# Linear attention's forget sums in two rounded passes, and attention's low weight halves one step later

## The chip, the cores and the metric

The kernel runs on one core of one Trainium2 chip. Time is device microseconds of one execution; lower is better. Before the change the median of 3 runs is 3329.88 us (3328.59 to 3332.18).

## The reference

Two transformer blocks follow one another on 512 tokens of width 1024. The first has 16 extra meta tokens (528 positions that count) and two layers. Each layer projects its input to four branches: windowed attention with a sink (A), attention with axial rotation (B), differential attention (C), and a gated linear attention (D) in both directions. Their outputs are weighed by gates and summed; a feed-forward follows. The second block has a feed-forward, attention with a state space model, and another feed-forward. The change touches only the first block; what matters of it:

```python
def gates(z, lb):
    f = lb + (1.0 - lb) * jax.nn.sigmoid(z)
    log_f = jnp.log(jnp.maximum(f, F_FLOOR))      # the forget logarithms
    kk = (1.0 - lb) * jax.nn.sigmoid(-z) * vmask
    return log_f, kk

def step(S, inp):                                  # one chunk of the linear attention
    qi, ki, vi, gi = inp                           # gi: log_f of the chunk
    b = jnp.cumsum(gi, axis=2)                     # sums of forget logarithms
    diff = b[:, :, :, None, :] - b[:, :, None, :, :]
    decay = jnp.where(tri, jnp.exp(jnp.where(tri, diff, 0.0)), 0.0)
    attn = jnp.einsum('bhtk,bhtsk,bhsk->bhts', qi, decay, ki)
    o = jnp.einsum('bhts,bhsv->bhtv', attn, vi) + jnp.einsum('bhtk,bhkv->bhtv', qi * jnp.exp(b), S)
    b_last = b[:, :, -1:, :]
    S = S * jnp.exp(b_last[:, :, 0, :, None]) + jnp.einsum('bhsk,bhsv->bhkv', ki * jnp.exp(b_last - b), vi)
    return S, o
```

## The kernel before

All engines have a program of their own, written out in order; semaphores join them. Nothing is scheduled by a planner: where an instruction stands in its engine's list is where the code puts it, by step numbers.

Most products are made in three rounded passes (type fp32r). A weight `w` is split into a high half, which ScalarE copies with rounding (`high_weights`, L1608), and a low half, which VectorE makes as weight minus high half (`low_weights`, L2026); inputs are split likewise. TensorE then adds high x high, high x low and low x high (L1040 to L1042; L1302 to L1304 for the gates). Unrounded fp32 matmuls appear as two records each in the trace.

A layer of the first block runs so:

1. Norm; then six products `fm[0..5]` with feature rows (weights w[0..5]). The first two are staged (`staged_lin`): all high x high first, then low weights, then low inputs. In layer 0 three small products for bias rows follow the second.
2. Products `tm` with token rows, for (i, t): i = 0, 1, 2 and five tiles t (four of 128 tokens, one of 16). ScalarE reads each from the accumulator (L1902 for i = 2). Tiles i = 0, 1 give the gates; GpSimd floors them; `forget_logs` runs on ScalarE in two passes over LZ (square root, L1851, and logarithm, L1848), after tiles 1 and 3 of i = 2.
3. Attention in steps n: first the C steps from c0, then A from a0, then B from b0. In a step TensorE makes scores, VectorE minima (L2147, L2163), ScalarE exponentials (L1679), TensorE turns and multiplies (L1205), ScalarE and VectorE copy and mix results (L1693, L2213); step n works on parts of attention n, n-1, n-2, n-3. The rest of the projections (weights w[12..21]) is put between as "fill" on TensorE, and their weights are split in given steps (`splits_at`), on ScalarE and VectorE in the same step n. From step b0+6 on, `gate_splits` prepares the first gate weights in the same way.
4. `linear_attention`: ten units (five tiles, two directions) per layer. In each, TensorE turns the keys (L1420), makes Z (L1422) and for each of two head pairs the `sums` (L1345): a matrix R of zeros and ones times the forget logarithms LZ, both fp32, with 128 rows and 2 x 512 columns. An exponential, the pair products on VectorE, and further small products follow. Between them stand gate pieces (`fill`).
5. Output product and feed-forward.

Of the kernel before, what the change touches and what calls it, by code (L numbers as in the profile page):

```python
# [23 lines left out]
P = 128  # L24
# [223 lines left out]
def build(nc, ins, out_dram):  # L248
    with ExitStack() as ctx:
# [134 lines left out]
        u6 = 4960  # L384
        XMH = [XR[:, base + (4 + i) * L:base + (5 + i) * L] for i in range(6)]
# [75 lines left out]
        names += """gate_floored dz_gate dz_log state_cleared g_sums g_exp g_kf g_query_x g_key_x g_z g_ez  # L461
# [126 lines left out]
        for l in range(DEPTH):  # L588
# [7 lines left out]
            for i, source in enumerate((FAQ, FAQ + 1, FCQ, FCQ + 1, FAK, FCK)):  # L596
                ly["w"].append(early(ins["w_fm"][l, source], KT, P))
                ly["fm"].append(split_job(ly["w"][-1], range(KT), 0, xu, FULL))
                if l == 0 and i == 1:
# [183 lines left out]
        for ly in layers:  # L783
# [5 lines left out]
            for n, i in ((c0 + 2, 14), (c0 + 3, 15), (a0, 16), (a0, 17), (a0 + 2, 18), (a0 + 3, 19), (b0, 20), (b0 + 1, 21)):  # L789
                splits_at.setdefault(n, []).append(ly["w"][i])  # L790
# [3 lines left out]
            split_from[ly["l"]] = b0 + 6  # L794

# [229 lines left out]
        def _(pe):  # L1025
# [291 lines left out]
            def linear_attention(ly):  # L1317
# [3 lines left out]
                pe.wait_ge(S["dz_log"], NT * (l + 1))  # L1321
# [18 lines left out]
                def sums(n, hp):  # L1340
# [73 lines left out]
                for n in range(NUNIT):  # L1414
# [51 lines left out]
            def first_block():  # L1466
                for ly in layers:
                    l = ly["l"]
                    mean_square(ly["norm"])
                    staged_lin(ly["fm"][0:2], ly["xu"])  # L1470
                    if l == 0:
                        bias_rows()
                    for j in ly["fm"][2:]:
                        split_lin(j)
# [99 lines left out]
        def _(act):  # L1574
# [159 lines left out]
            def attention(first, end, ly=None):  # L1734
                for n in range(first, end + 2):
# [130 lines left out]
            def first_block():  # L1866
                for ly in layers:
                    l = ly["l"]
                    if l == 0:
                        squares(ly["norm"])  # L1870
                        for ld in ly["w"][0:2]:
                            high_weights(ld)
                    else:
                        root(ly["norm"])
                        act.wait_ge(S["h_stored"], 64)
                    high_tiles(ly["xu"])
                    high_weights(ly["w"][2])
                    for i, j in enumerate(ly["fm"]):
# [9 lines left out]
                        if l == 0 and i in (1, 3, 5):  # L1888
                            (bias_rows, start_exp, start_lambda)[i // 2]()
# [3 lines left out]
                    for i, t, j in ly["tm"]:  # L1893
                        full(act, j)
                        acc_t, c = PB[j.buf][0:j.rows, 0, 0:CG], CG * (i % 3)
                        if i < 2:
                            A(KTM[0:j.rows, t, c:c + CG], acc_t, ACT.Sigmoid, scale=-1.0)
                            A(LZ[0:j.rows, t, c:c + CG], acc_t, ACT.Sigmoid).then_inc(S["tm_ready"], 1)
                            if (i, t) in ((0, 1), (1, 2), (1, 3)):
                                high_weights(ly["w"][(9, 8 + t)[i]])  # L1900
                            continue
# [892 lines left out]
```

## Time and profile before

| | |
|---|---|
| median of 3 runs | 3329.88 us |
| profiled execution, its own time | 3336.33 us |
| its span | 3334.2 us |
| mean granted TensorE clock | 0.955 |
| TensorE busy | 3094.7 us (93%) |
| VectorE busy | 1771.0 us (53%) |
| ScalarE busy | 1006.5 us (30%) |
| GpSimd busy | 218.8 us (7%) |
| L1345 (sums), 128 rows | 66.1 us busy, 128 records |

The span is the profiled execution's, and its own time contains a little more around it. Busy time of TensorE is modelled at the ends of matmuls, so that neighbours overlap in the rows; the distance from one start to the next is what a matmul holds the engine. A window row gives the length of a stretch and what each engine was busy in it, with the clock granted to TensorE (1.00 is full speed).

### The profile page before, as it was taken

How to read it: one execution, taken by the hardware profiler on the slowest of the kernel's cores; microseconds unless marked ns; L12 is line 12 of the kernel's file. 1: busy time of each engine (PE TensorE's matmuls, PEld its weight loads, DVE VectorE, ACT ScalarE, POOL GpSimd, SP SyncE). 2: the span in 40 equal slices, each digit the busy share in tenths (PEclk: the TensorE clock that was granted, in tenths of full speed). 3: DMA queues.
4: the chain of work that ended last, by engine and by line, in shares of the span. 5: the costliest groups of instructions: out<-in, count | busy, mean ns of one | idle time of the engine just before them, and what ended most of it. 6: DMA issues, size and time to landing. Idle time of an engine off the chain costs nothing.

```text
span 3334.2 us, 51815 instructions
## 1 busy us (share of the span) xinstructions
PE 3094.7 (93%) x21724; PEld 2610.9 (78%) x21724; DVE 1771.0 (53%) x3315; ACT 1006.5 (30%) x1728; POOL 218.8 (7%) x455
## 2 busy tenths in 40 slices
PE   8888999999999998889999999989999797889997
PEld 7766888999999896778888788867888454558886
DVE  4463476547646436446755775646446425453334
ACT  4554222232212235432223222233222114332221
POOL 0120211100000100212110000000000000000000
PEclk9988899999999999989999999989999898899998
DMA  5201111134534420111114453412334210213231
GB/s 180 88 14 45 41 57 57 64 129 146 175 106 130 134 72 31 38 41 57 57 56 138 149 177 122 149 60 89 114 113 170 91 45 1 70 59 105 89 102 69
DMA packets 74494, 302.47 MB, mean 91 GB/s; under 512 B 10728, under 2 KB 11112, under 8 KB 69272
## 3 DMA queue, kind: packets, MB, share of 16 engines
q1 hardware_dynamic: 57880, 230.04, 21.4%
q0 software_dynamic: 16384, 69.13, 5.8%
q8 instruction: 173, 2.83, 0.4%
q14 instruction: 57, 0.47, 0.0%
HBM read 288.51 MB, written 14.63 MB: 91 GB/s over the span
## 4 chain that ended last, share of the span: by engine, by line
PE 84%; DVE 9%; ACT 5%; issue 2%; DMA 0%; POOL 0%; DVEq 0%; ACTq 0%; SPq 0%
PE acc L1040 17%; PE acc L1041 17%; PE acc L1042 17%; PE acc L1302 5%; PE acc L1303 5%; PE acc L1304 5%; PE acc L1074 3%; PE acc L1345 2%; PE acc L1205 2%; PE acc L1179 1%; DVE work L1975 1%; ACT temps L1679 1%; DVE normed L1993 1%; PE acc L1366 1%; PE acc L1089 1%
## 5 line engine op out<-in xcount | busy, mean ns | idle before, releaser
L1041 PE MATMUL acc<-normed_r,toep_r 128*128 128x512 f32 (+1 forms) x1824 | 644.2, 353 | 0.0
L2026 DVE TENSOR_TENSOR ring_r<-ring,toep_r 128x1024 fp32r<-128x1024 f32 (+2 forms) x340 | 458.6, 1350 | 298.2 <-ACT toep_r L1608 297.8
L1608 ACT ACTIVATE toep_r<-ring 128x1024 fp32r<-128x1024 f32 (+2 forms) x340 | 392.7, 1157 | 710.4 <-PE acc L1042 709.6
L1041 PEld LDWEIGHTS acc<-normed_r,toep_r 128*128 128x128 f32 x1824 | 345.5, 189 | 46.2 <-issue 0.2
L1040 PE MATMUL acc<-work_r,toep_r 128*128 128x512 f32 (+1 forms) x1024 | 354.0, 346 | 6.5 <-DVE temps_r L2017 6.3
L1042 PE MATMUL acc<-work_r,ring_r 128*128 128x512 f32 (+1 forms) x1024 | 353.0, 345 | 0.0
L1040 PE MATMUL acc<-mixed_r,toep_r 128*128 128x264 f32 (+1 forms) x1056 | 343.9, 326 | 5.1 <-DVE ring_r L2026 4.4
L1042 PE MATMUL acc<-mixed_r,ring_r 128*128 128x264 f32 (+1 forms) x1056 | 340.1, 322 | 0.0
L1040 PE MATMUL acc<-temps_r,toep_r 128*128 128x512 f32 x768 | 305.0, 397 | 24.3 <-DVE normed_r L2012 14.8
L1302 PE MATMUL acc<-residual_r,toep_r 128*128 128x264 f32 (+1 forms) x1024 | 316.0, 309 | 1.6 <-DVE mixed L2213 1.6
L1041 PE MATMUL acc<-work_r,toep_r 128*128 128x512 f32 (+1 forms) x880 | 307.3, 349 | 0.0
L1042 PE MATMUL acc<-temps_r,ring_r 128*128 128x512 f32 x768 | 302.1, 393 | 0.0
L1303 PE MATMUL acc<-normed_r,toep_r 128*128 128x264 f32 (+1 forms) x1024 | 293.6, 287 | 0.0
L1304 PE MATMUL acc<-residual_r,ring_r 128*128 128x264 f32 (+1 forms) x1024 | 292.3, 285 | 0.0
L1040 PEld LDWEIGHTS acc<-work_r,toep_r 128*128 128x128 f32 x1024 | 192.7, 188 | 31.9 <-issue 6.9
L1040 PEld LDWEIGHTS acc<-mixed_r,toep_r 128*128 128x128 f32 x1056 | 200.0, 189 | 20.2 <-issue 5.2
L1042 PEld LDWEIGHTS acc<-mixed_r,ring_r 128*128 128x128 f32 x1056 | 200.2, 190 | 15.7
L1042 PEld LDWEIGHTS acc<-work_r,ring_r 128*128 128x128 f32 x1024 | 192.9, 188 | 24.4
L1302 PEld LDWEIGHTS acc<-residual_r,toep_r 128*128 128x128 f32 x1024 | 197.5, 193 | 15.4 <-issue 8.5
L1303 PEld LDWEIGHTS acc<-normed_r,toep_r 128*128 128x128 f32 x1024 | 197.2, 193 | 7.9 <-issue 7.9
L1304 PEld LDWEIGHTS acc<-residual_r,ring_r 128*128 128x128 f32 x1024 | 197.4, 193 | 0.0
L1040 PEld LDWEIGHTS acc<-temps_r,toep_r 128*128 128x128 f32 x768 | 145.5, 189 | 64.5 <-issue 25.1
(389 smaller groups left out, 5438.1 us busy)
## 6 DMA issues: line engine op xcount, KB each, us to landing
ring<-in_w_pair SPq DMA_DIRECT2D x176, 512.0 KB, 3.5
ring<-in_w_down SPq DMA_DIRECT2D x64, 704.0 KB, 4.1
ring<-in_w_gb SPq DMA_DIRECT2D x64, 640.0 KB, 3.9
extra<-in_w_ada POOLq DMA_DIRECT2D x18, 1024.0 KB, 5.7
toep<-in_w_ada POOLq DMA_DIRECT2D x18, 1024.0 KB, 5.5
ring<-in_w_tm SPq DMA_DIRECT2D x24, 512.0 KB, 3.8
ring<-in_w_out SPq DMA_DIRECT2D x24, 512.0 KB, 3.5
ring<-in_w_fm SPq DMA_DIRECT2D x20, 512.0 KB, 4.0
```

Of the source, the lines that this page charges most:

```text
L1040: mm(out, wh, xh[:, a:z], start=i == 0, stop=False)
L1041: mm(out, wh, xl[:, a:z], start=False, stop=False)
L1042: last = mm(out, wl, xh[:, a:z], start=False, stop=end)
L1074: last = mm(PB[j.buf][0:j.rows, s, 0:z - a], w, x[:, a:z], start=i == 0, stop=i == len(j.terms) - 1)
L1089: last = mm(n["acc"][:, s, :], mean[P * len(n["tiles"])], x[:, a:z], start=i == 0, stop=i == len(n["tiles"]) - 1)
L1205: last = mm(PS[64 * j:64 * j + 64, 6, P * i:P * i + rows], v, x, start=b == 0, stop=b == k - 1, skip_group_check=True)
L1302: mm(out, wh, xh[:, a:z], start=m == 0, stop=False)
L1303: mm(out, wh, xl[:, a:z], start=False, stop=False)
L1304: last = mm(out, wl, xh[:, a:z], start=False, stop=m == len(xs) - 1)
L1345: last = mm(PS[:, i, :].rearrange("p (l t) -> p l t", l=4)[:, :, 0:rows], LZ[0:rows, t, 256 * d + P * hp:256 * d + P * hp + P], R[d][0:row ...
L1608: A(high(ld), slot(ld), ACT.Copy).then_inc(S["w_high"], 1)
L2026: V.tensor_tensor(low(ld), slot(ld), high(ld), ALU.subtract).then_inc(S["w_low"], 1)
```

## The change

- `sums` and `Z` take the logarithms as a high half LZH and a low half LZL and the 0/1 matrices in rounded type: two rounded passes for each matmul. The matrices are rounded in place by ScalarE once, in layer 0 (two copies of 128x1152). The log halves are made by `high_log` (ScalarE) in steps b0+1 to b0+5, and `low_log` (VectorE) one step later, five tiles each.
- Low weight halves and the low parts of `gate_splits` are made on VectorE one attention step after the high halves. w[16] and w[17] are split a step earlier on ScalarE (a0-1).
- `forget_logs` stands after tiles 0 and 2, and the splits of w[12] and w[13] after tiles 1 and 2.
- At a layer's start three products are staged; bias rows follow the third; w[2] is split with w[0] and w[1] (layer 0), or before the root and the tiles (layer 1).

```diff
@@ tensor engine @@
-                    staged_lin(ly["fm"][0:2], ly["xu"])
+                    staged_lin(ly["fm"][0:3], ly["xu"])
...
                     for i in range(2):
-                        last = mm(PS[:, i, :].rearrange("p (l t) -> p l t", l=4)[:, :, 0:rows],
-                                  LZ[0:rows, t, 256 * d + P * hp:256 * d + P * hp + P],
-                                  R[d][0:rows, 4 * i:4 * i + 4, 0:rows], start=True, stop=True)
+                        for x in (LZH, LZL):
+                            last = mm(PS[:, i, :].rearrange("p (l t) -> p l t", l=4)[:, :, 0:rows],
+                                      x[0:rows, t, 256 * d + P * hp:256 * d + P * hp + P],
+                                      RR[d][0:rows, 4 * i:4 * i + 4, 0:rows], start=x is LZH, stop=x is LZL)
                     last.then_inc(S["g_sums"], 1)
...
-                    mm(PS[0:rows, 5, 0:256], Z[d][0:rows, 0:rows], LZ[0:rows, t, 256 * d:256 * d + 256],
-                       start=True, stop=True).then_inc(S["g_z"], 1)
+                    mm(PS[0:rows, 5, 0:256], ZR[d][0:rows, 0:rows], LZH[0:rows, t, 256 * d:256 * d + 256],
+                       start=True, stop=False)
+                    mm(PS[0:rows, 5, 0:256], ZR[d][0:rows, 0:rows], LZL[0:rows, t, 256 * d:256 * d + 256],
+                       start=False, stop=True).then_inc(S["g_z"], 1)
@@ attention steps @@
-            for n, i in ((c0 + 2, 14), (c0 + 3, 15), (a0, 16), (a0, 17), (a0 + 2, 18), (a0 + 3, 19), (b0, 20), (b0 + 1, 21)):
+            for n, i in ((c0 + 2, 14), (c0 + 3, 15), (a0 - 1, 16), (a0 - 1, 17), (a0 + 2, 18), (a0 + 3, 19), (b0, 20), (b0 + 1, 21)):
+            ly["log_step"] = b0 + 1
@@ scalar engine @@
+                    if ly and 0 <= n - ly["log_step"] < NT:
+                        high_log(ly["l"], n - ly["log_step"])
...
+            def high_log(l, t):
+                n = TILES[t][1] - TILES[t][0]
+                act.wait_ge(S["dz_log"], NT * l + t + 1)
+                A(LZH[0:n, t, :], LZ[0:n, t, :], ACT.Copy).then_inc(S["log_high"], 1)
...
-                        for ld in ly["w"][0:2]:
+                        for ld in ly["w"][0:3]:
                             high_weights(ld)
                     else:
+                        high_weights(ly["w"][2])
                         root(ly["norm"])
                         act.wait_ge(S["h_stored"], 64)
                     high_tiles(ly["xu"])
-                    high_weights(ly["w"][2])
...
-                        if t in (2, 3):
-                            high_weights(ly["w"][10 + t])
-                        if t in (1, 3):
-                            forget_logs(l, t == 3)
+                        if t in (1, 2):
+                            high_weights(ly["w"][11 + t])
+                        if t in (0, 2):
+                            forget_logs(l, t == 2)
@@ vector engine @@
-                    for ld in splits_at.get(n, ()) if n < end else ():
+                    for ld in splits_at.get(n - 1, ()) if first < n <= end else ():
                         low_weights(ld)
-                    if ly and n >= split_from[ly["l"]]:
+                    if ly and 0 <= n - 1 - ly["log_step"] < NT:
+                        low_log(ly["l"], n - 1 - ly["log_step"])
+                    if ly and n > split_from[ly["l"]]:
                         for i in range(2 + ly["l"]):
-                            gate_splits(ly, (n - split_from[ly["l"]]) * (2 + ly["l"]) + i)
+                            gate_splits(ly, (n - 1 - split_from[ly["l"]]) * (2 + ly["l"]) + i)
+
+            def low_log(l, t):
+                n = TILES[t][1] - TILES[t][0]
+                dve.wait_ge(S["log_high"], NT * l + t + 1)
+                V.tensor_tensor(LZL[0:n, t, :], LZ[0:n, t, :], LZH[0:n, t, :], ALU.subtract).then_inc(S["log_low"], 1)
```

TensorE (PE) in the first unit of the linear attention, before:

```order
L1420 MATMUL acc<-con,extra 128x128 x2
L1422 MATMUL acc<-work,con 128x256
L1345 MATMUL acc<-con,work 128x512 x2
L1302 MATMUL acc<-residual_r,toep_r 128x264
L1303 MATMUL acc<-normed_r,toep_r 128x264
```

The same place now:

```order
L1429 MATMUL acc<-con,extra 128x128 x2
L1431 MATMUL acc<-work_r,con_r 128x256
L1433 MATMUL acc<-work_r,con_r 128x256
L1354 MATMUL acc<-con_r,work_r 128x512 x4
L1309 MATMUL acc<-residual_r,toep_r 128x264
L1310 MATMUL acc<-normed_r,toep_r 128x264
```

One exact matmul of Z became two rounded ones, and two exact ones of the sums four; the gate pieces behind them stand where they stood.

VectorE (DVE) in the C step in which w[14] is split (L2147 minima, L2183 and L2197 the mix of the step before, L2026 the low half), before:

```order
L2147 ISA temps,small<-acc,toep,small 128x512
L2147 ISA small 128x1
L2026 TENSOR_TENSOR ring_r<-ring,work_r 128x1024
L2183 RECIPROCAL small<-small 128x4
L2186 SCALAR_TENSOR_TENSOR small<-small 128x2
L2197 SCALAR_TENSOR_TENSOR temps<-temps,small 128x528 x2
L2163 SCALAR_TENSOR_TENSOR temps<-acc,toep 128x2x16 x2
L2171 TENSOR_REDUCE small<-temps 128x4
L2147 ISA temps,small<-acc,toep,small 128x512
```

Now (L2171 minima, L2207 and L2221 the mix, L2050 the low half):

```order
L2171 ISA temps,small<-acc,toep,small 128x512
L2171 ISA small 128x1
L2207 RECIPROCAL small<-small 128x4
L2210 SCALAR_TENSOR_TENSOR small<-small 128x2
L2221 SCALAR_TENSOR_TENSOR temps<-temps,small 128x528 x2
L2187 SCALAR_TENSOR_TENSOR temps<-acc,toep 128x2x16 x2
L2195 TENSOR_REDUCE small<-temps 128x4
L2171 ISA temps,small<-acc,toep,small 128x512
...
L2050 TENSOR_TENSOR ring_r<-ring,work_r 128x1024
L2237 TENSOR_TENSOR mixed<-mixed,acc 128x2x128
```

The low half left its place ahead of the next step's reciprocal and stands behind that step's last minimum.

ScalarE (ACT) at the end of the token-major products (L1902 the reads, L1608 a high half, L1848 the pass of logarithms), before:

```order
L1902 ACTIVATE work<-acc 128x256
L1608 ACTIVATE mixed_flat_r<-ring 128x1024
L1902 ACTIVATE work<-acc 128x256
L1608 ACTIVATE mixed_flat_r<-ring 128x1024
L1848 ACT_TABLE_LOAD
L1848 ACTIVATE work<-work 128x512 x4
L1848 ACTIVATE work<-work 16x512
L1902 ACTIVATE work<-acc 16x256
```

Now (L1926 the reads, L1619 a high half, L1867 the logarithms):

```order
L1926 ACTIVATE work<-acc 128x256
L1619 ACTIVATE mixed_flat_r<-ring 128x1024
L1926 ACTIVATE work<-acc 128x256
L1619 ACTIVATE mixed_flat_r<-ring 128x1024
L1867 ACT_TABLE_LOAD
L1867 ACTIVATE work<-work 128x512 x4
L1867 ACTIVATE work<-work 16x512
L1926 ACTIVATE work<-acc 128x256
L1926 ACTIVATE work<-acc 16x256
```

Two reads stand behind the logarithms in place of one, the one of the last whole tile and the one of the tile of 16 rows.

## Rows read from the trace of the kernel before

**Rows 1.** The page, the chain that ended last, share of the span by engine.

```profile
PE 84%; DVE 9%; ACT 5%; issue 2%; DMA 0%; POOL 0%; DVEq 0%; ACTq 0%; SPq 0%
```

**Rows 2.** Windows: length, then busy and (count) of PE, PEld, DVE, ACT, POOL; clock.

```profile
116.20:342.50 226.30, 195.33 (x1719) 152.17 (x1719) 117.52 (x362) 116.17 (x323) 24.72 (x25) 0.88 0.09 29
343.00:618.00 275.00, 264.62 (x2866) 233.96 (x2866) 173.30 (x386) 71.74 (x115) 51.48 (x146) 0.96 0.17 54
...
1446.00:1718.00 272.00, 260.85 (x2891) 230.38 (x2889) 175.10 (x387) 72.62 (x117) 50.62 (x145) 0.96 0.17 55
```

**Rows 3.** Lines by form, PE: busy and mean ns, idle before.

```profile
L1345 PE MATMUL acc<-con,work 128*128 128x512 f32 x128 | 66.1, 642 | 0.0
```

**Rows 4.** Timeline of PE in the linear attention: start, length.

```profile
431.43 0.60 PE L1422 MATMUL acc<-work,con 128*128 128x256 f32 x2
431.87 1.88 PE L1345 MATMUL acc<-con,work 128*128 128x512 f32 x4
433.18 0.69 PE L1302 MATMUL acc<-residual_r,toep_r 128*128 128x264 f32 x1
...
433.83 0.28 PE L1304 MATMUL acc<-residual_r,ring_r 128*128 128x264 f32 x1
433.95 0.28 PE L1302 MATMUL acc<-residual_r,toep_r 128*128 128x264 f32 x1
```

**Rows 5.** Timeline of PE in the second block's feed-forward.

```profile
2500.14 0.39 PE L1041 MATMUL acc<-normed_r,toep_r 128*128 128x512 f32 x1
2500.37 0.39 PE L1042 MATMUL acc<-temps_r,ring_r 128*128 128x512 f32 x1
```

**Rows 6.** Timeline of PE, another block of sums.

```profile
402.73 3.30 PE L1345 MATMUL acc<-con,work 128*128 128x512 f32 x4
405.36 0.79 PE L1302 MATMUL acc<-residual_r,toep_r 128*128 128x264 f32 x1
```

**Rows 7.** Windows of C steps, the second to fourth with a split.

```profile
130.28:137.25 6.97, 6.85 (x66) 5.48 (x65) 5.04 (x15) 4.48 (x14) 0.00 (x0) 1.00 0.00 0
137.25:148.22 10.97, 8.71 (x73) 7.48 (x72) 6.18 (x16) 5.97 (x17) 0.00 (x0) 0.84 0.01 1
148.22:159.13 10.91, 8.00 (x66) 5.74 (x65) 7.13 (x20) 5.92 (x15) 0.00 (x0) 0.84 0.00 0
...
1280.69:1291.96 11.27, 8.36 (x65) 5.93 (x64) 7.49 (x20) 5.92 (x15) 0.00 (x0) 0.85 0.00 0
```

**Rows 8.** Timelines of DVE and PE there; in brackets the wait and its releaser.

```profile
139.08 1.23 DVE L2026 TENSOR_TENSOR ring_r<-ring,work_r 128x1024 fp32r<-128x1024 f32 x1 [3.47 <-ACT work_r L1608]
142.47 0.38 PE L1176 MATMUL acc<-con,temps 128*16 128x128 f32 x2 [2.26 <-DVE temps L2163]
158.43 0.18 DVE L2183 RECIPROCAL small<-small 128x4 f32<-128x4 f32 x1 [1.78 <-ACT temps L1679]
```

**Rows 9.** Timeline of PE, A steps of the first and the second layer.

```profile
220.23 0.52 PE L1179 MATMUL acc<-con,temps 128*128 128x128 f32 x3 [1.91 <-ACT mixed L1693]
1335.32 0.66 PE L1205 MATMUL acc<-mixed,work 128*64 128x128 f32 x8 [1.57 <-DVE mixed L2213]
```

**Rows 10.** Windows of B steps.

```profile
277.96:288.14 10.18, 8.31 (x62) 7.08 (x61) 3.10 (x9) 4.42 (x11) 0.00 (x0) 0.83 0.22 66
288.14:295.29 7.15, 7.15 (x70) 5.99 (x69) 2.30 (x8) 3.39 (x9) 0.00 (x0) 1.00 0.00 0
1392.93:1401.98 9.05, 6.76 (x61) 5.53 (x60) 3.33 (x9) 4.60 (x11) 0.00 (x0) 1.00 0.25 74
...
323.19:332.22 9.03, 7.11 (x38) 3.82 (x37) 3.40 (x10) 4.33 (x11) 0.00 (x0) 0.50 0.00 0
```

**Rows 11.** Timeline of PE, start of the second layer's attention.

```profile
1249.94 0.43 PE L1145 MATMUL acc<-con,work 128*128 128x64 f32 x2 [2.88 <-ACT work L1902]
```

**Rows 12.** Timeline of PE, first products of the first and the second layer.

```profile
45.02 0.39 PE L1040 MATMUL acc<-residual_r,temps_r 128*128 128x264 f32 x1 [1.09 <-ACT work L1840]
1159.81 1.12 PE L1059 MATMUL acc<-residual_r,temps_r 128*128 128x264 f32 x2 [5.97 <-ACT residual_r L1623]
```

More of the change, by code:

```diff
@@ L384, in build @@
         u6 = 4960
+        LZH, LZL = (x.rearrange("p (t c) -> p t c", t=NT) for x in (
+            XR[:, base + 4 * L:base + 4 * L + NT * 512], XR[:, z0:z0 + NT * 512]))
+        sums_at = CONSTS["R0"][0], CONSTS["Z1"][1]
+        con_r = rounded("con")
+        RR = [part(con_r, CONSTS, f"R{d}").rearrange("p (l t) -> p l t", l=8) for d in range(2)]
+        ZR = [part(con_r, CONSTS, f"Z{d}") for d in range(2)]
         XMH = [XR[:, base + (4 + i) * L:base + (5 + i) * L] for i in range(6)]
@@ L598, in build @@
                 ly["fm"].append(split_job(ly["w"][-1], range(KT), 0, xu, FULL))
-                if l == 0 and i == 1:
+                if l == 0 and i == 2:
                     bias_jobs = [job([(part(par, PARAMS, "bias_tab", 32),
@@ L1320, in linear_attention @@
                 pe.wait_ge(S["y_ready"], ly["groups"])
-                pe.wait_ge(S["dz_log"], NT * (l + 1))
+                pe.wait_ge(S["sums_rounded"], 2)
+                pe.wait_ge(S["log_low"], NT * (l + 1))
                 pe.wait_ge(S["fill_read"], NFILL * (l + 1))
@@ L1469, in first_block @@
                     mean_square(ly["norm"])
-                    staged_lin(ly["fm"][0:2], ly["xu"])
+                    staged_lin(ly["fm"][0:3], ly["xu"])
                     if l == 0:
                         bias_rows()
-                    for j in ly["fm"][2:]:
+                    for j in ly["fm"][3:]:
                         split_lin(j)
@@ L1887, in first_block @@
                         high_weights(ly["w"][i + 3])
-                        if l == 0 and i in (1, 3, 5):
-                            (bias_rows, start_exp, start_lambda)[i // 2]()
+                        if l == 0 and i in (2, 3, 5):
+                            (bias_rows, start_exp, start_lambda)[(i - 1) // 2]()
                     if l == 0:
@@ L1900, in first_block @@
                                 high_weights(ly["w"][(9, 8 + t)[i]])
+                            if l == 0 and (i, t) in ((0, 2), (0, 3)):
+                                act.wait_ge(S["consts_loaded"], 16)
+                                m = sums_at[0] + (t - 2) * (sums_at[1] - sums_at[0]) // 2
+                                w = slice(m, m + (sums_at[1] - sums_at[0]) // 2)
+                                A(con_r[:, w], con[:, w], ACT.Copy).then_inc(S["sums_rounded"], 1)
                             continue
                         A(TMt[0:j.rows, t, TAV:TAV + CG], acc_t, ACT.Copy).then_inc(S["tm_ready"], 1)
-                        if t in (2, 3):
-                            high_weights(ly["w"][10 + t])
-                        if t in (1, 3):
-                            forget_logs(l, t == 3)
+                        if t in (1, 2):
+                            high_weights(ly["w"][11 + t])
+                        if t in (0, 2):
+                            forget_logs(l, t == 2)
                     attention(ly["C"][0], ly["B"][1], ly)
@@ L2441, in start @@
                 V.tensor_tensor(lb, lb, lo, ALU.subtract).then_inc(S["lb_shift"], 1)
-                for ld in w[5:7]:
-                    low_weights(ld)
+                low_weights(w[6])
                 dve.wait_ge(S["lb_exp"], 1)
@@ L2696, in first_block @@
                     normed(ly["norm"], gain("ln_mix", l), U)
-                    if l == 0:
-                        for ld in ly["w"][0:2]:
-                            low_weights(ld)
+                    for ld in ly["w"][2 * l:3]:
+                        low_weights(ld)
                     low_tiles(ly["xu"])
-                    for ld in ly["w"][2:5]:
+                    for ld in ly["w"][3:6 - l]:
                         low_weights(ld)
```

2 lines of the change are left out of this document (1 added, 1 removed).

## The prediction

> **What bounds the kernel now.** I read first the chain of waits: 84% of the span is TensorE work, 9% VectorE, 5% ScalarE, and DMA is at 0% [rows 1]. So only what TensorE does, or what it waits for, can move the time. Then the windows by stage. In the linear attention of either layer TensorE is busy 264.62 of 275.00 us and 260.85 of 272.00, with VectorE at 173.30 and ScalarE at 71.74 [rows 2]: that stage ends with TensorE's own work, and a cheaper matmul there is worth its whole length as long as the others keep up. In the attention stage TensorE is busy 195.33 of 226.30 us [rows 2], so some 30 us per layer are waits, each followed by a stretch at a lower granted clock (0.88 over the stage). There it matters which instruction TensorE stands behind. The change touches both: cheaper sums in the first, another order of VectorE's work in the second. The queues of SyncE and GpSimd keep their order.
>
> **Part 1, the sums.** The kernel runs 128 records of L1345 with 512 columns, of 642 ns mean by the modelled ends [rows 3]; since ends are modelled I go by starts. One block of `sums` (two matmuls, four records) starts at 431.87 and what follows starts at 433.18, and the next weight-and-row group comes only at 433.95 [rows 4]. The first matmul behind the block then holds 0.77 us instead of the 0.37 that three passes of 264 columns take at 0.12 each (433.83 to 433.95) [rows 4]. So a block holds TensorE 1.31 + 0.40 = 1.71 us; as four equal records, 4 x 0.43 = 1.72. In the new kernel it is four rounded matmuls of 512 columns. One of those takes 0.23 from start to start (2500.14 to 2500.37) [rows 5]: 0.92 a block, 0.80 less. There are 32 such blocks; 28 run at full clock: 28 x 0.80 = 22.4. Four run at half (402.73 to 405.36, 2.63 us, twice the 1.31 [rows 6]) and save about 1.35 each: 5.4. Together 27.8. `Z` was two records of 256 columns in 0.44 us (431.43 to 431.87) [rows 4] and becomes two rounded ones of half of 0.23 each, 0.24: 0.2 x 16 units = 3.1. The units of 16 rows I count at 0.5 in all, as they are an eighth of the size. Linear attention: **-31.4**. Bounds: -34.6 if a block holds TensorE for the whole 1.88 us of its row (0.96 x 32 = 30.7 in place of 27.8), and +62 if a rounded pass takes as long as two exact records (rival D).
>
> TensorE would be late if the pairs on VectorE came to set the pace. They use 173.30 of 275.00 us [rows 2]; with 31.4/2 = 16 less per layer there remain about 259, still 86 above VectorE's work.
>
> On this the Trainium skill has a rule that speaks against it ("TensorE: Matmul & The Clock Gate", LDWEIGHTS (loading the stationary operand)): a load takes its columns / 1.2 in ns, an estimated 107 ns for 128 columns; were every load to show, the sum would be about 17 us smaller (4 x 0.107 x 32 + 2 x 0.107 x 16). The trace disagrees that it shows: rounded passes of 264 columns, each with a load, follow one another in 0.12 us [rows 4].
>
> **Part 2, low halves one step late.** A C step without a split lasts 6.97 us, with TensorE busy 6.85. The steps in which w14 and w15 are split last 10.97, 10.91 and, in layer 1, 11.27, at clock 0.84 or 0.85 [rows 7] (the fourth is like the first). The cause stands in rows 8: the low half starts on VectorE at 139.08 after 3.47 us of waiting for ScalarE's high half, which closes its own step; everything queued behind it (reciprocal, difference, the next minima) is late by that, and TensorE idles 2.26 us at 142.47, and then pays half clock. In the changed kernel the high half was made a step earlier, so VectorE starts it without a wait. Its own 1.23 us remain, but VectorE waits 1.78 us for ScalarE's exponentials at 158.43 anyway [rows 8], and this hides it. Four steps x (10.97 - 7.0): **-15.9**. Bounds: 0 (the wait reappears at another releaser) to -16.5.
>
> The same in the A steps: four waits of the kind of 1.91 and 1.57 us [rows 9], 6.5 in all with their clock. Half of them end with ScalarE's copies (L1693) and not with VectorE, so I take two thirds: **-4.3** (0 to -6.5). The high halves of w16 and w17 also go a step earlier on ScalarE, into the last C step; a plain one has it busy for 4.48 of 6.97 us [rows 7], so two copies fit.
>
> B steps: 10.18 against a plain 7.15 is 3.0; the step before it gives 1.2, layer 1 gives 1.9 (9.05) and 0.3 [rows 10]: **-6.4** (0 to -6.4). Gate splits at the end of B: the step of 323.19 lasts 9.03 at clock 0.50, TensorE busy 7.11 [rows 10], so 1.92 idle. Two steps of either layer are of this kind: 4 x 1.92 = **-7.7** (-2, as some of it is the end of the attention itself, to -12 with the half clock).
>
> Against that: the log halves. ScalarE copies five tiles of 512 per layer in steps b0+1 to b0+5, VectorE subtracts five, one step later. A subtraction of 1024 elements takes 1.23 us [rows 8], so half of it, 0.6 or a bit more. The Trainium skill gives for fp32 of 512 elements an estimate of (512+151)/0.96 = 691 ns ("VectorE: DVE Perf Modes", The TRN2 errata); by it the five would be 3.5 us, hidden or not as below. A plain B step has VectorE busy 2.30 and ScalarE 3.39 of 7.15 us [rows 10], so the work is covered; what is queued behind it, the first minimum or exponential of the next step, may come late by some of it. 0.2 x 10 = **+2.0** (0 to +7, if all is on the path).
>
> **Part 3, forget logs.** ScalarE's pass of logarithms (a table load and five activations) stands before the last reads of the projections, and TensorE waits 2.88 us at 1249.94 for the read behind it [rows 11], and as long in layer 0. One tile earlier, two reads follow the pass and TensorE has a tile's matmuls left meanwhile: I leave it one read's wait, an estimated 0.45, so 2 x 2.43 = **-4.8** for both layers (0 to -5.8). It now needs the floor of the gates earlier, but only one tile's time.
>
> **Part 4, starts and rounding.** In layer 0 three products are staged by halves instead of two, and ScalarE copies w[2] before the tiles. TensorE waits 1.09 at 45.02 for the bias rows' copies [rows 12]; afterwards the bias rows come one product later and w[5]'s DMA is what is waited for there: 0 (-1 to +2). In layer 1 w[2]'s high half is now before the root on ScalarE, in the chain whose end is TensorE's longest wait, 5.97 us at 1159.81 [rows 12]: **+1.0** (0 to +1.1), the 1.06 us of such a copy. The rounding of the constants (two copies of 1152 columns) is in layer 0's token-major tiles, where ScalarE has over 2 us idle per tile: 0 (to +2.3).
>
> **Sum.** -31.4 - 15.9 - 4.3 - 6.4 - 7.7 + 2.0 - 4.8 + 1.0 = -67.5. The profiled execution took 3336.33 (its span is 3334.2), so 3268.8; the median of the runs is 6.45 below it: **3262**. For this case alone I take 3252 to 3278: not all terms reach their ends together.
>
> **Rivals.** A: the waits move rather than go. VectorE's low half now stands before the step's last minima or mixes, ScalarE's exponentials become the releaser, and only a third of part 2's 34.3 is had: 23 less, **3285**. For it: ScalarE is busy 5.97 of 10.97 in a C step [rows 7] and is the releaser at 158.43. Against: plain steps of the same kind reach 6.97 with both engines.
> B: shorter sums run into the chain sums, exp, pairs, products; linear attention gives only a third, 10.5: **3283**. For it: `pairs` come directly on the sums' exp. Against: 86 us of room, and behind a block stands gate work (L1302 to L1304), not a reader of the sums [rows 4].
> C: loads show. Each rounded pass with another stationary operand pays up to a 0.12 on top: a block 1.40 instead of 0.92, 15 us, and Z another 4: **3281**. [...]
> D, the other side: rounded does not take effect in these shapes (strided output, 4 blocks of the 0/1 matrix), and each of the new matmuls costs two records: a block 3.44 instead of 1.72 (32 x 1.72 = 55), Z 0.88 instead of 0.44 (7): +62 in place of -31.4. The rest gives -36.1, so +26, **3356**. It decides from 0.68 us a rounded pass of 512 columns on, where 144 such passes (128 of the sums, Z's as 16) cost 98, the 62 of before and the 36 that the rest saves. Against it: 0.23 for rounded 512 columns [rows 5].
>
> **Chances.** Forecast 0.62, A 0.18, B 0.10, C 0.06, D 0.03, and 0.01 for a sum of near nothing. Range 3250 to 3292: it takes in A, B and C, leaves out D and the tails. What this kernel's measurement can tell from no change is 0.2%, 6.7 us. Faster 0.96, within 0.01, slower 0.03.
>
> **What would show it.** Four records of the sums from start to next start 0.9 us, and in the linear attention about 259 us of window. C steps with splits at 7 to 7.5 us and clock near 1.0; no wait of 2.88 at the attention's start; the wait at the start of layer 1 at 7.0. I am wrong if a C step stays over 9 us, if VectorE's subtractions of the logs make B steps 8 us or longer, or if the block of sums holds TensorE over 1.2 us.

## The result and the profile after

The changed kernel takes 3255.27 us in the median of 4 runs (3252.83 to 3257.44), against 3329.39 us for the kernel before (4 runs, 3328.59 to 3332.18): ratio 0.9776, 95% interval 0.9759 to 0.9793. The forecast was 3262, its range 3250 to 3292. The gain is 74.1 us; the forecast was 67.5.

The page of the changed kernel, its head and the chain that ended last; it answers to [rows 1]:

```profile
span 3253.3 us, 51837 instructions
...
PE 83%; DVE 9%; ACT 5%; issue 2%; POOL 0%; DMA 0%; DVEq 0%; ACTq 0%; SPq 0%
```

The kernel is bound as it was. The two profiled spans differ by 80.9 us, 6.8 more than the medians do. Part of that is placed below, in the run with part 1 alone: in two places the profile of before shows a lower clock and a longer time than other profiles of the same instructions.

Windows of the changed kernel: layer 0's attention and linear attention with all gate pieces, then the same for layer 1 (length; busy time and count of PE, PEld, DVE, ACT, POOL; clock; DMA share and GB/s):

```profile
117.39:319.99 202.60, 181.51 (x1720) 142.44 (x1720) 120.16 (x368) 117.66 (x329) 24.56 (x25) 0.96 0.10 35
319.99:657.64 337.65, 326.18 (x3502) 310.24 (x3503) 204.91 (x438) 90.75 (x145) 55.93 (x148) 0.95 0.18 61
...
1207.80:1387.09 179.29, 162.63 (x1503) 129.70 (x1504) 103.51 (x298) 104.50 (x274) 24.98 (x25) 0.99 0.11 39
1387.09:1713.57 326.48, 315.23 (x3490) 299.66 (x3490) 204.38 (x437) 90.16 (x145) 55.15 (x147) 0.97 0.19 63
```

Cut at the same instructions, the kernel before has 226.32, 354.94, 200.26 and 342.43 us. So attention became 23.7 + 21.0 = 44.7 us shorter, and the linear attention 17.3 + 16.0 = 33.3. The clock of layer 0's attention rose from 0.88 [rows 2] to 0.96.

The sums, timeline of TensorE in the unit that answers to [rows 4]:

```profile
402.79 0.37 PE L1431 MATMUL acc<-work_r,con_r 128*128 128x256 f32 x1
402.99 0.28 PE L1433 MATMUL acc<-work_r,con_r 128*128 128x256 f32 x1
403.11 1.10 PE L1354 MATMUL acc<-con_r,work_r 128*128 128x512 f32 x4
404.05 0.28 PE L1309 MATMUL acc<-residual_r,toep_r 128*128 128x264 f32 x1
404.17 0.28 PE L1310 MATMUL acc<-normed_r,toep_r 128*128 128x264 f32 x1
```

A block of sums now lasts 0.94 us (403.11 to 404.05), and the pass behind it 0.12 (404.05 to 404.17) instead of 0.5. Z takes 0.32 (402.79 to 403.11) instead of 0.44.

The C steps that answer to [rows 7]: a plain one, the two of layer 0 with a split, and the second of layer 1:

```profile
130.25:137.22 6.97, 6.84 (x65) 5.48 (x64) 5.04 (x15) 4.47 (x14) 0.00 (x0) 1.00 0.00 0
137.22:144.31 7.09, 7.09 (x73) 5.90 (x73) 6.18 (x16) 5.54 (x16) 0.00 (x0) 1.00 0.01 2
144.31:152.55 8.24, 6.99 (x65) 4.88 (x65) 6.51 (x17) 5.55 (x14) 0.00 (x0) 1.00 0.00 0
1234.70:1242.95 8.25, 6.93 (x65) 4.86 (x64) 6.51 (x17) 5.56 (x14) 0.00 (x0) 1.00 0.00 0
```

VectorE in the step that begins at 137.22; it answers to [rows 8]:

```profile
142.46 1.22 DVE L2050 TENSOR_TENSOR ring_r<-ring,work_r 128x1024 fp32r<-128x1024 f32 x1
145.40 0.42 DVE L2237 TENSOR_TENSOR mixed<-mixed,acc 128x256 f32<-128x256 f32 x1 [1.72 <-ACT mixed L1713]
```

The low half has no wait in brackets any more (it was 3.47), and VectorE waits 1.72 us behind it: the subtraction now lies in time in which VectorE would have been idle (a hole). TensorE is busy for all 7.09 us of that step.

B steps answer to [rows 10]: the one of w[21]'s high half in layer 0, the step behind it (with w[21]'s low half and halves of the logarithms), the step that answers to 323.19, and w[21]'s in layer 1. The last row is layer 1's end of the attention:

```profile
266.72:273.41 6.69, 6.69 (x62) 5.53 (x61) 2.06 (x8) 4.93 (x12) 0.00 (x0) 1.00 0.31 100
273.41:280.55 7.14, 7.14 (x70) 5.98 (x69) 3.94 (x10) 3.79 (x10) 0.00 (x0) 1.00 0.00 0
305.10:310.23 5.13, 3.96 (x38) 2.25 (x37) 4.19 (x11) 4.20 (x12) 0.00 (x0) 1.00 0.00 0
1338.16:1345.20 7.04, 6.76 (x62) 5.53 (x61) 2.20 (x8) 5.13 (x12) 0.00 (x0) 1.00 0.28 95
1371.75:1387.09 15.34, 10.80 (x101) 7.43 (x101) 6.71 (x14) 8.74 (x20) 0.00 (x0) 0.89 0.00 1
```

The last one has this counterpart before, from the same instruction to the same (window of the kernel before):

```profile
1428.41:1450.20 21.79, 13.27 (x101) 9.31 (x101) 6.79 (x14) 8.97 (x20) 0.00 (x0) 0.68 0.00 1
```

Here the same 101 records of TensorE take 2.47 us less busy time, at a clock of 0.89 instead of 0.68, and the idle time falls from 8.52 to 4.54. A log's low half on VectorE, in a B step:

```profile
287.64 0.43 DVE L2160 SCALAR_TENSOR_TENSOR work<-work,acc 128x264 f32<-128x264 f32 x1 [3.85 <-ACT work L1743]
287.99 0.68 DVE L2284 TENSOR_TENSOR work_r<-work,work_r 128x512 fp32r<-128x512 f32 x1
```

It takes 0.68 us, where VectorE was idle for 3.85 us just before. Last the starts, TensorE at the attention's start of layer 1 (answers to [rows 11]), at the first products of layer 1, and at the first product behind the bias rows of layer 0 (both to [rows 12]):

```profile
1207.80 0.44 PE L1152 MATMUL acc<-con,work 128*128 128x64 f32 x2 [0.46 <-ACT work L1926]
...
1120.67 0.56 PE L1066 MATMUL acc<-residual_r,temps_r 128*128 128x264 f32 x1 [6.92 <-ACT residual_r L1634]
...
51.72 0.59 PE L1047 MATMUL acc<-residual_r,temps_r 128*128 128x264 f32 x1 [1.56 <-ACT work L1859]
52.11 0.42 PE L1048 MATMUL acc<-normed_r,temps_r 128*128 128x264 f32 x1
52.33 0.42 PE L1049 MATMUL acc<-residual_r,ring_r 128*128 128x264 f32 x1
```

The first wait fell by 2.42, the second rose by 0.95. The third is 1.56 for 1.09, and what is new stands behind it: the passes start 0.22 apart and not 0.12, which is half clock, until 57.8.

### The profile page after: what moved, and what is told of

Read it like the earlier page. It is cut to its first block, busy times and chain, and to the rows that moved or that the text cites. A ratio compares the mean times of both kernels' runs of the same rounds, so it can differ in the third digit from the quotient of the medians.

```text
span 3253.3 us, 51837 instructions
## 1 busy us (share of the span) xinstructions
PE 3037.7 (93%) x21724; PEld 2591.9 (80%) x21724; DVE 1775.1 (55%) x3325; ACT 1011.7 (31%) x1740; POOL 220.4 (7%) x455
## 4 chain that ended last, share of the span: by engine, by line
PE 83%; DVE 9%; ACT 5%; issue 2%; POOL 0%; DMA 0%; DVEq 0%; ACTq 0%; SPq 0%
PE acc L1047 18%; PE acc L1048 17%; PE acc L1049 17%; PE acc L1309 5%; PE acc L1310 5%; PE acc L1311 5%; PE acc L1081 3%; ACT temps L1690 2%; PE acc L1212 2%; DVE work L1999 1%; PE acc L1066 1%; PE acc L1354 1%; PE acc L1186 1%; DVE normed L2017 1%; PE acc L1375 1%
## 5 line engine op out<-in xcount | busy, mean ns | idle before, releaser
L1619 ACT ACTIVATE toep_r<-ring 128x1024 fp32r<-128x1024 f32 (+2 forms) x340 | 392.7, 1157 | 711.4 <-PE acc L1049 710.6
L2050 DVE TENSOR_TENSOR ring_r<-ring,toep_r 128x1024 fp32r<-128x1024 f32 (+2 forms) x340 | 458.1, 1348 | 263.6 <-ACT toep_r L1619 263.3
L1309 PE MATMUL acc<-residual_r,toep_r 128*128 128x264 f32 (+1 forms) x1024 | 302.1, 295 | 1.6 <-DVE mixed L2237 1.6
```

The lines of the kernel that those rows point to most:

```text
L1309: mm(out, wh, xh[:, a:z], start=m == 0, stop=False)
L1619: A(high(ld), slot(ld), ACT.Copy).then_inc(S["w_high"], 1)
L2050: V.tensor_tensor(low(ld), slot(ld), high(ld), ALU.subtract).then_inc(S["w_low"], 1)
```

## The experiments

The experiments ran in three sets, each with runs of the kernel before on the same chip; its medians were 3332.11, 3332.64 and 3330.98 us. The third set (part 1 alone, and all behind it) ran on another chip and has no run of the changed kernel. The changed kernel has ratio 0.9776 and, once more in the second set, 0.9765. A ratio's interval is some 0.0015 to either side, 5 us, so differences of that size are read from the stages of the profiles. A stage is measured from one instruction of TensorE to another; in most stages where code and clock are the same the lengths agree within 0.1 us. Each kernel has one profile, the changed one two, so a stretch at lower clock in one profile can be chance of that execution.

**Part 1 undone.** Both exact matmuls back, no log halves, no rounded constants:

```diff
-                        for x in (LZH, LZL):
-                            last = mm(..., x[...], RR[d][...], start=x is LZH, stop=x is LZL)
+                        last = mm(..., LZ[...], R[d][...], start=True, stop=True)
```

> The changed kernel with part 1 undone: sums and Z exact on the unsplit logarithms, no log halves, no rounded constants. Forecast's theory (a rounded block holds TensorE 0.92 us instead of 1.72): 31 to 33 us longer than the changed kernel, near 3287, all of it in the two linear attention stages (gate pieces to their end 338 and 326 us become 355 and 342), and the B steps as they are, at 7.14, if the log halves were hidden; B steps 0.2 shorter each if they were not. Rival B (the chain of pairs sets the pace): 10 us longer only.

Measured: 3287.07 us, ratio 0.9864 (0.985 to 0.9879), 0.0088 and 0.0099 above the two of the changed kernel, 29 to 33 us. Windows of the two linear attention stages:

```profile
318.43:672.46 354.03, 343.51 (x3502) 311.75 (x3503) 205.83 (x438) 90.74 (x145) 55.38 (x148) 0.96 0.18 58
1403.60:1744.30 340.70, 330.55 (x3491) 299.86 (x3489) 204.85 (x437) 89.93 (x145) 54.82 (x148) 0.97 0.19 60
```

They are 16.4 and 14.2 us longer. Layer 0's attention has 202.57 us (changed kernel 202.60) and its B steps 7.14 as with the halves: the ten halves of the logarithms cost nothing that shows. (Layer 1's attention is even 0.7 longer without them, at a clock of 0.98 for 0.99.) Rival B, by which the linear attention would give only a third, is out.

**Low weight halves in their step again.**

```diff
-                    for ld in splits_at.get(n - 1, ()) if first < n <= end else ():
+                    for ld in splits_at.get(n, ()) if n < end else ():
```

and w[16], w[17] at a0 again.

> The changed kernel with the low halves of w[14] to w[21] again in the step of their high halves (w[16], w[17] in a0 again); gate splits and log halves stay one step late. Theory: C steps with a split return to 10.9 to 11.3 us, B steps to 8.3, 10.2 and 9.1; sum of the measured step differences of these steps 13 + 8 + 8, so 29 us longer, near 3284. Rival (the waits were only half the splits' and also the shorter stretches at low clock of the other parts): under 15 us.

Measured: 3285.11 us, ratio 0.9858 (0.9841 to 0.9874), 0.0082 and 0.0093 above the two of the changed kernel, 27 to 31 us. The attention stages are 12.7 and 17.0 us longer. Windows of the two C steps of layer 0 and of layer 1's w[21] step, and VectorE in the first of them:

```profile
136.26:146.93 10.67, 8.73 (x73) 7.48 (x72) 6.17 (x16) 5.65 (x14) 0.00 (x0) 0.84 0.01 2
146.93:159.29 12.36, 9.61 (x65) 6.47 (x65) 8.35 (x21) 5.91 (x15) 0.00 (x0) 0.72 0.00 0
...
1363.55:1375.56 12.01, 9.72 (x62) 8.11 (x61) 3.34 (x9) 5.12 (x12) 0.00 (x0) 0.72 0.17 56
...
137.78 1.23 DVE L2050 TENSOR_TENSOR ring_r<-ring,work_r 128x1024 fp32r<-128x1024 f32 x1 [3.56 <-ACT work_r L1619]
```

The wait of VectorE is back (3.56), and the C steps are long again with one line undone, so this wait for a half just ordered is their cause. Step by step the expectation was met only in the sum: the C steps take 10.67, 12.36, 9.79 and 12.64 us (10.9 to 11.3 expected), the B steps 6.79 and 8.65 in layer 0 (8.3 and 10.2 expected) and 12.01 for w[21] in layer 1 (9.1 expected). Rival A, by which the waits only move, is out.

**Gate splits in their step again.**

```diff
-                    if ly and n > split_from[ly["l"]]:
-                            gate_splits(ly, (n - 1 - split_from[ly["l"]]) * (2 + ly["l"]) + i)
+                    if ly and n >= split_from[ly["l"]]:
+                            gate_splits(ly, (n - split_from[ly["l"]]) * (2 + ly["l"]) + i)
```

> The changed kernel with the low parts of the gate splits at the end of B again in the step of their high parts. Theory: the end of the attention in layer 0 and 1 gets 7.9 and 6.5 us longer, 14 in all, near 3269, twice the 7.7 of the prediction. Rival (most of the 14 came from elsewhere, such as the log halves' place or the clock left by earlier steps): 8 or less.

Measured: 3273.81 us, ratio 0.9828 (0.9813 to 0.9842), 0.0052 and 0.0063 above the two of the changed kernel, 17 to 21 us, where 14 were expected. Windows: the two steps of layer 0 that answer to 299.89 and 305.10, and layer 1's end:

```profile
300.21:308.29 8.08, 4.48 (x45) 2.89 (x44) 4.67 (x9) 5.09 (x11) 0.00 (x0) 1.00 0.00 0
308.29:316.79 8.50, 6.49 (x38) 3.49 (x36) 3.40 (x10) 4.20 (x12) 0.00 (x0) 0.60 0.00 0
...
1379.87:1401.67 21.80, 13.28 (x101) 9.33 (x101) 6.80 (x14) 8.97 (x20) 0.00 (x0) 0.69 0.00 1
```

The attention stages are 9.1 and 6.5 us longer. Of the 9.1, 7.1 are the end of B, so the two ends give 13.6, near the 14 expected; layer 1's takes 21.80 us, as before the change. Layer 1's linear attention is 3.2 longer too, with no instruction changed, at a clock of 0.95 for 0.97 (see the last section).

**Layer 0's start as before.**

```diff
-                    staged_lin(ly["fm"][0:3], ly["xu"])
+                    staged_lin(ly["fm"][0:2 + l], ly["xu"])
```

with the bias rows after i == 1, w[2] and its halves where they were.

> The changed kernel with layer 0's start as before: two staged products, bias rows after the second, w[2] high after the tiles. Layer 1 keeps the new start. Theory (the new start of layer 0 costs 3.3 us: a wait of 1.56 instead of 1.09 and 28 matmuls at half clock behind it): 3.3 us shorter, near 3252. Rival (the half clock falls elsewhere whatever the order, as a wait by w[5] remains): within 1 us.

Measured: 3253.46 us, ratio 0.9763 (0.9748 to 0.9777). The start, from the first product to the attention, is 3.65 us shorter (89.64 for 93.29), and layer 0's attention 2.97 longer (205.57 for 202.60), with the same code: its second step takes 8.65 instead of 7.44 and its twelfth 9.53 instead of 8.52. In this profile the gain is mostly given back by stretches of half clock that fall on other steps; against the second profile of the changed kernel (next) the start is 2.25 shorter and the attention 2.43 longer.

**The changed kernel again.**

> The changed kernel itself once more, as the mark for the next three. 0.9776 of the kernel before; stages as in its first profile within 0.4 us, but for the first steps of layer 0's attention, where a stretch of half clock may fall on other steps (up to 3 us).

Measured: 3254.31 us, ratio 0.9765 (0.9752 to 0.9779). Stages within 1.4 us of the first profile in layer 0 (start 91.89 for 93.29, linear attention 338.63 for 337.65), within 0.1 in layer 1. The 0.4 us expected for all stages but the attention's first steps was too narrow: the same code differs by 1.4 in a start, where the half clock now ends at 53.9 and not at 57.8.

**Bias rows' copies first.**

```diff
+                        if l == 0 and i == 2:
+                            bias_rows()
                         high_weights(ly["w"][i + 3])
-                        if l == 0 and i in (2, 3, 5):
+                        if l == 0 and i in (3, 5):
```

> The changed kernel with ScalarE's copies of the bias rows in layer 0 ahead of the high half of w[5] instead of behind it. Theory (the wait of 1.56 us at 51.72 is the copies' wait behind w[5]'s DMA, and the half clock behind it costs 2.8 more): the stretch from the first product to the attention 3 to 4 us shorter, 89.6 as with two staged products. Rival (TensorE must then wait for w[5] itself or for the low half): no gain.

Measured: 3252.62 us, ratio 0.9759 (0.9746 to 0.9772). The start takes 89.43 us, 2.5 to 3.9 less than the changed kernel's two profiles. ScalarE and TensorE there:

```profile
48.06 0.84 ACT L1859 ACTIVATE work<-acc 8x389 f32<-8x389 f32 x2
...
49.45 1.04 ACT L1619 ACTIVATE temps_r<-ring 128x1024 fp32r<-128x1024 f32 x1
```

```profile
48.95 0.39 PE L1047 MATMUL acc<-residual_r,temps_r 128*128 128x264 f32 x1
49.18 0.28 PE L1048 MATMUL acc<-normed_r,temps_r 128*128 128x264 f32 x1
```

There is no wait before the product and no half clock behind it. The attention of layer 0 is 1.1 to 1.7 longer again, and in the total the gain can't be told from nothing (3252.62 against 3254.31 us).

**w[2] behind the root in layer 1.**

```diff
-                        high_weights(ly["w"][2])
                         root(ly["norm"])
+                        high_weights(ly["w"][2])
```

> The changed kernel with layer 1's high half of w[2] behind the root instead of ahead of it, on ScalarE. Theory (the copy of 1.04 us stands in the chain root, norm, first product): the norm stretch of layer 1 goes from 9.92 to 8.97 us and the sum gets 1.0 shorter, the projections unchanged. Rival (the copy then delays the tiles' high halves as much): no change.

Measured: 3257.93 us (5 runs, 3252.47 to 3262.83), ratio 0.9777 (0.9763 to 0.979), no gain. The norm does take 8.97 us instead of 9.92; then the projections take 0.46 more, the attention 0.47, and the linear attention 3.0. Windows of the linear attention's last two parts between the same waits, first the changed kernel run again, then this one:

```profile
1435.23:1594.78 159.55, 157.91 (x1932) 147.76 (x1933) 119.12 (x257) 47.99 (x75) 33.80 (x96) 0.99 0.20 63
1594.78:1712.99 118.21, 111.59 (x1035) 108.22 (x1036) 57.90 (x120) 28.12 (x45) 9.29 (x21) 0.93 0.19 64
```

```profile
1434.07:1595.50 161.43, 159.78 (x1932) 149.62 (x1933) 119.10 (x257) 48.03 (x75) 33.84 (x97) 0.98 0.19 63
1595.50:1714.87 119.37, 112.77 (x1036) 109.40 (x1037) 57.89 (x120) 28.15 (x45) 9.28 (x21) 0.91 0.19 64
```

In the first of the two there are 1932 records and the same waits, but 1.87 us more of busy TensorE, at a clock of 0.98 for 0.99; idle time is 1.64 and 1.65. The 3.0 us are no fixed price of the edit: the last run below has the same edit, and there the linear attention takes 326.52, as in the changed kernel.

**Forget logarithms as before.**

```diff
-                        if t in (0, 2):
-                            forget_logs(l, t == 2)
+                        if t in (1, 3):
+                            forget_logs(l, t == 3)
```

with the splits of w[12] and w[13] one tile later.

> The changed kernel with part 3 undone: the passes over the forget logarithms after tiles 1 and 3, splits of w[12] and w[13] after tiles 2 and 3. Theory: the wait at the attention's start returns from 0.46 to 2.88 us in both layers, 4.8 us longer in all, near 3260. Rival (the table load and the exponentials that follow set the first C step, whatever stands before): under 1.5 us.

Measured: 3259.94 us, ratio 0.9786 (0.9773 to 0.98), 5.6 us above the changed kernel of the same set, in the medians, where 4.8 were expected; the intervals overlap, so the waits say more. TensorE at layer 0's attention start:

```profile
117.05 0.43 PE L1152 MATMUL acc<-con,work 128*128 128x64 f32 x2 [2.87 <-ACT work L1926]
```

In layer 1 it is 2.88. Both waits of the kernel before are back.

**Part 1 alone on the kernel before.** Here the kernel before gets what the first experiment took away: rounded sums and Z and the halves of the logarithms; parts 2 to 4 are as before.

> The kernel before with part 1 alone: rounded two-pass sums and Z, log halves (the low ones one step later), constants rounded; weight and gate splits, forget passes and starts as before. Theory (the parts add): 30 us shorter than before, near 3302, linear attention stages at 338 and 327 to 330 us, the B steps with logs at 7.14 and no longer. Rival (the gain of part 1 needs the free VectorE of part 2; B steps with log halves grow by 0.7 each when waits stand there): 3 to 7 us less.

Measured: 3302.89 us, ratio 0.9908 (0.989 to 0.9927), which is 30.6 us by the ratio and 28.1 between the medians of this set. The linear attention stages take 339.13 and 330.46 us, 15.8 and 12.0 less than before, and the B steps behind w[21]'s stay at 7.14. Within the interval (24 to 37 us) the parts add. That interval can't exclude the rival's loss of 3 us, but its mechanism is out, as no B step with log halves grew. This profile also has the attention of layer 0, in its old order, at 222.72 us and not 226.32: the step that answers to 323.19 [rows 10] and the one of w[20] are here

```profile
321.82:328.56 6.74, 4.82 (x38) 2.27 (x36) 3.40 (x10) 4.11 (x10) 0.00 (x0) 0.84 0.00 0
269.75:276.54 6.79, 6.18 (x58) 5.24 (x57) 3.01 (x8) 3.74 (x10) 0.00 (x0) 1.00 0.00 0
```

2.29 and 1.54 us shorter than in the profile of before (9.03 and 8.33), with clocks of 0.84 and 1.00. And the last stage of the second block takes 480.4 us in this and all other profiles, 483.4 in that of before. 3.6 + 3.0 has the size of the 6.45 us by which that profiled run lay above its median. It isn't a full account: just behind layer 1's linear attention the profile of before is up to 1.6 us shorter than this one, so that all that follows that stage is only 1.4 us longer in it.

**The sums' low pass left out; made twice.**

```diff
-                        for x in (LZH, LZL):
+                        for x in (LZH,):
```

```diff
-                        for x in (LZH, LZL):
+                        for m, x in enumerate((LZH, LZL, LZL)):
```

> The changed kernel with the sums' low pass left out (only the high halves of the logarithms are summed; Z keeps both). 64 passes of 512 columns fewer at 0.23 us, 8 of them at half clock, so 17 us, and 16 small ones. Theory (TensorE sets the pace of the linear attention still): 14 to 17 us shorter, near 3238. Rival B (the chain of exponential and pairs is next): under 8 us.

> The changed kernel with the sums' low pass made twice (the sums get the low halves doubly). 64 passes of 512 columns more. Theory (a rounded pass costs 0.23 us, its load hidden): 15 to 17 us longer, near 3271. Rival C (a load shows behind each pass, 0.35): 22 us or more. At 0.43, as an exact record: 28.

The start and stop flags follow. Measured: 3239.95 us, ratio 0.9721 (0.9705 to 0.9737), and 3272.25 us, ratio 0.9821 (0.9804 to 0.9838): some 0.005 below and above the changed kernel; by its two medians 14 to 15 us less and 17 to 18 us more. The block with six records:

```profile
406.42 1.56 PE L1354 MATMUL acc<-con_r,work_r 128*128 128x512 f32 x6
407.82 0.28 PE L1309 MATMUL acc<-residual_r,toep_r 128*128 128x264 f32 x1
```

1.40 us for six is 0.233 each, against the 0.35 of rival C, so no load shows and rival C is out. The Trainium skill ("TensorE: Matmul & The Clock Gate", Back-to-back issue gap) gives 512/2.4 + 2.5 = 216 ns for one matmul by itself, which is 7% below this, and some 131 ns for 512 columns in a sustained stream, which no rounded matmul here comes near (the shortest distance between starts in the changed kernel is 0.22 us); the measurement decides. By starts, the 32 blocks with the three passes behind each take 46.6 us in the changed kernel, 30.3 without the low pass and 62.9 with two of it: 16.3 to either side. The two stages of the linear attention became 12.8 us shorter and 19.0 longer. So the passes taken away don't come off in full there; but TensorE's idle time in these stages grows by only 1.1 us (22.7 to 23.8), so it sets the pace even then.

**Both starts.**

```diff
+                        if l == 0 and i == 2:
+                            bias_rows()
...
-                        high_weights(ly["w"][2])
                         root(ly["norm"])
+                        high_weights(ly["w"][2])
```

> The changed kernel with the bias rows' copies ahead of w[5]'s high half and w[2]'s high half of layer 1 behind the root. By the stage rows of the two alone: 2.5 and 1.0 us shorter directly, and stretches of half clock that fall elsewhere give back 1 to 4 us of it. Near 3252, within 0.2% of the changed kernel.

Measured: 3251.56 us, ratio 0.9758 (0.9741 to 0.9775). Of the kernels that sum both halves once it has the lowest median and the shortest profiled span (3247.5), and it is well ahead of the kernel before; from the changed kernel the intervals can't tell it. Its start takes 88.39 us, its first attention 202.67.

## Why the prediction was right

**The sums and Z (-31.4): right.** The stages gave 33.3; undone it is 30.6 of stage (16.4 + 14.2), and alone 27.8 of stage and 30.6 by the ratio. The mechanism is as forecast: a block with the three passes behind it took 1.32 + 0.77 and takes 0.94 + 0.36. Not as forecast is that only 14 of the 32 blocks are of this kind; 14 others take 1.01 to 1.04, which I had not seen, and four at half clock 1.71. All 32 with the passes behind them went from 72.5 to 46.6 us, 25.9 in place of the 27.8 of my sum. Z gave 3.7, the turns of the keys ahead of it, for which I had no term, 1.5; the sums of the 16-row units cost 1.6 more, where I had these units at a gain of 0.5 in all. Some 2.6 of the 33.3 are no gain of part 1: the profile with the exact sums back is that much shorter in these two stages than the profile of before. My lower bound of -34.6 was added up wrongly; its terms give -34.3. I left loads out of the sum by the 0.12 of the passes of 264 columns, and the 0.233 per pass of 512 bears this out. D, two records per rounded pass, is excluded by the same rows.

**C steps (-15.9): 13.4.** Step by step 3.89, 2.66, 3.86 and 3.02. The second of each pair does not go to 7.0 but to 8.24: every second C step has about this length, with a split or without. Two steps of the kernel before in which no weight is split (windows):

```profile
166.22:174.29 8.07, 6.99 (x66) 5.51 (x65) 5.38 (x16) 4.44 (x12) 0.00 (x0) 1.00 0.01 3
181.42:189.61 8.19, 6.94 (x66) 5.16 (x64) 5.33 (x16) 4.60 (x14) 0.00 (x0) 1.00 0.01 2
```

I took one plain step of 6.97 as the floor for all, where steps of 7.1 and 8.1 to 8.2 take turns.

**A steps (-4.3): 7.9**, beyond my bound of 6.5. 1.24 and 1.21 in layer 0, 1.23, 1.21 and 3.04 in layer 1. I took a third off since the releaser named was ScalarE's copy L1693. But with the low halves in their step again four of these five steps took 5.27, 7.51, 8.79 and 10.49 (changed kernel 4.29, 6.28, 6.06, 8.14; the fifth stayed, 12.51 for 12.50), ahead of the same copies: the name of the releaser was no evidence that the wait would stay.

**B steps (-6.4): 8.1**, of which 1.5 is the step that was at low clock only in the profile of before. It is beyond my bound of 6.4: w[21]'s step in layer 0 went to 6.69, below the plain 7.15 that I had as its floor. **End of B (-7.7): 14.3**, the term that was most off. 7.85 in layer 0, of it 2.3 by the clock of that profile; 6.45 in layer 1. I counted idle time of one step, and left out what followed it: the stretch at half clock. The window of 1428.41 shows it: 4.0 us of the gain are idle time and 2.5 are clock. My bound of 12 named the half clock, and the value chosen did not hold it; 14.3 lies outside even that bound, and 12.0 without the 2.3. With the gate splits in their step again the two ends got 13.6 us longer, so the term is the gate splits' own.

Part 2 as a whole was forecast at 34.3 and gave 43.8, of which 3.8 are the two steps of the profile of before. So its mechanism holds, and its size was set too low.

**Log halves (+2.0): 0.** B steps 7.14 with them, 7.15 without. **Forget logs (-4.8): right**, 2 x 2.42 of wait. **Layer 1's start (+1.0): right**, 0.95. **Rounding the constants (0):** without it, in the first experiment, the start of layer 0 takes 92.78, between the changed kernel's 91.89 and 93.29. **Layer 0's start (0): wrong by 1.9 to 3.3.** The start went from 92.36 to 93.29 or 91.89, though the forget logs took 2.42 out of it. I had put the bias rows' copies behind w[5]'s transfer and seen no more than a wait of the same length. The wait is about as long (1.56 for 1.09), but half clock follows it now, to 57.83, and behind the wait of before the passes went on at 0.12. With the copies first both are gone (89.43). This is the same omission as at the end of B, with the other sign.

The sum of the terms was 67.5 and the medians gave 74.1. The 6.6 between them is the net of errors of both signs: part 2 and the log halves came out better than their terms, layer 0's start worse. The profiled run of before lay 6.45 us above its median, which I took off; 3.8 of such time stood in rows that I priced.

## What to carry over

When an engine is to finish what another engine starts, give it to it one step after the order, into a hole that the profile shows; a wait in a queue that keeps its order costs its length, delays the work behind it, and can be followed by a stretch of TensorE at half clock. Price such a wait by the whole window from its step to where the clock is back at full. Take as the floor a step of the same place in the pattern (in the C steps here 7.1 and 8.2 take turns), not just any plain step. A releaser that is itself waiting is not the cause. Where TensorE sets the pace, count its records by their starts, and include the one behind.

## What the hardware showed

The same instructions took different times by where stretches of half clock fell: layer 0's attention 202.6 to 205.6 us, and layer 1's linear attention with rounded sums 326.5 in six profiles, 328.7 to 330.5 in four. Some stretches came with short waits (1.56 us ahead of 51.72, 2.26 us ahead of 142.47 in the kernel before), but the 1.09 us ahead of 45.02 had none behind it. So a gain of 1 us at a start can be seen in its stage and be absent in the total, as in the run with w[2] behind the root.

One might think that a wait removed early only moves the half clock to a later step, as the run with two staged products and the one with the bias copies first suggest. Other runs don't bear this out: those with the weight splits and with the gate splits undone have half clock both in layer 0's start and in the first steps of its attention, and the run with both starts mended has it in neither (88.39 and 202.67 us). What decides on which step such a stretch falls stays open; no run here was made for it.
